# Gate and up product of a SwiGLU block moved from VectorE to ScalarE and GpSimd

## What is computed

```python
gate, up = _split(rms_norm(x, norm_ffn[i]) @ w_gate_up[i], (D_FF, D_FF))   # 2048 -> 2 * 5632
x = x + (jax.nn.silu(gate) * up) @ w_down[i]                               # 5632 -> 2048
```

## Time and profile before

| | us |
|---|---|
| median of 3 runs | 2177.11 (2175.9 to 2177.83) |
| the profiled execution | 2178.24 |
| its span, first to last instruction | 2176.4 |
| TensorE busy (share of the span) | 2158.2 (99%) |
| VectorE busy | 1555.4 (71%) |
| ScalarE busy | 1095.3 (50%) |
| GpSimd busy | 58.4 (3%) |

### The profile page before, as it was taken

The page is one execution under the profiler, slowest core; times in us unless marked ns, Lnnn a source line. Parts: engine busy times, 40 slices in busy tenths (PEclk is TensorE's granted clock), DMA queues, the critical chain, the costliest instruction groups (busy, mean ns, idle before and its releaser), DMA issues.

```text
span 2176.4 us, 29853 instructions
## 1 busy us (share of the span) xinstructions
PE 2158.2 (99%) x10052; PEld 1784.3 (82%) x10052; DVE 1555.4 (71%) x1937; ACT 1095.3 (50%) x1414; POOL 58.4 (3%) x99
## 2 busy tenths in 40 slices
PE   8999999999999999999999999999999999999999
PEld 6888888888888888888888888888878888888887
DVE  6657766888888885555566767677888888874443
ACT  7755654545555554444444444454454545544332
POOL 2101100000000000000100000000000000000000
PEclk9999999999999999999999999999999999999999
DMA  8765466667666666666555656566676666666664
GB/s 313 233 194 155 138 211 204 202 194 222 202 206 214 214 217 199 205 205 202 177 172 164 202 158 191 172 206 209 195 221 203 205 208 217 201 219 218 202 203 133
DMA packets 244569, 435.57 MB, mean 200 GB/s; under 512 B 23040, under 2 KB 43648, under 8 KB 244480
## 3 DMA queue, kind: packets, MB, share of 16 engines
q1 hardware_dynamic: 243392, 432.31, 63.7%
q10 hardware_dynamic: 1088, 2.10, 0.2%
HBM read 411.25 MB, written 2.10 MB: 190 GB/s over the span
## 4 chain that ended last, share of the span: by engine, by line
PE 70%; DVE 11%; issue 7%; SPq 6%; DMA 4%; ACT 2%; DVEq 1%; ACTq 0%
PE unit_bank L1801 52%; SPq L408 5%; PE mix_bank L1853 4%; PE mix_bank L1801 4%; DMA raw<-in_w_gate_up 4%; PE unit_bank L1853 3%; DVE w_lo L1074 3%; PE unit_bank L1813 1%; PE mix_bank L1813 1%; PE mix_bank L1871 1%; DVE sums L1096 1%; ACT w_hi L615 1%; PE mix_bank L2001 1%; DVE up_ff L1574 1%; DVE act_ff L1598 1%
## 5 line engine op out<-in xcount | busy, mean ns | idle before, releaser
L1074 DVE TENSOR_TENSOR w_lo<-raw,w_hi 128x1024 fp32r<-128x1024 f32 x687 | 828.8, 1220 | 472.8 <-ACT w_hi L615 450.7
L615 ACT ACTIVATE w_hi<-raw 128x1024 fp32r<-128x1024 f32 x687 | 719.0, 1057 | 603.4 <-PE unit_bank L1801 381.9
L1801 PE MATMUL unit_bank<-w_hi,gT_hi 128*128 128x512 f32 x704 | 217.1, 389 | 1.3 <-issue 1.3
L1801 PE MATMUL unit_bank<-w_lo,gT_hi 128*128 128x512 f32 x704 | 216.9, 389 | 0.0
L1801 PE MATMUL unit_bank<-w_hi,gT_lo 128*128 128x512 f32 x704 | 216.8, 389 | 0.0
L1801 PE MATMUL unit_bank<-w_hi,hT_hi 128*128 128x512 f32 (+1 forms) x576 | 181.2, 396 | 0.0
L1801 PE MATMUL unit_bank<-w_hi,hT_lo 128*128 128x512 f32 (+1 forms) x576 | 176.2, 387 | 0.0
L1801 PE MATMUL unit_bank<-w_lo,hT_hi 128*128 128x512 f32 (+1 forms) x576 | 175.9, 387 | 0.0
L1801 PEld LDWEIGHTS unit_bank<-w_hi,gT_hi 128*128 128x128 f32 x704 | 132.0, 188 | 29.4 <-issue 2.0
L1801 PEld LDWEIGHTS unit_bank<-w_lo,gT_hi 128*128 128x128 f32 x704 | 132.2, 188 | 27.5
L1801 PEld LDWEIGHTS unit_bank<-w_hi,gT_lo 128*128 128x128 f32 x704 | 132.2, 188 | 27.4
(11 more groups left out here) (348 smaller groups left out, 3113.9 us busy)
## 6 DMA issues: line engine op xcount, KB each, us to landing
raw<-in_w_gate_up SPq DMA_DIRECT2D x352, 512.0 KB, 4.2
raw<-in_w_down SPq DMA_DIRECT2D x176, 512.0 KB, 4.6
raw<-in_w_in_b SPq DMA_DIRECT2D x104, 512.0 KB, 4.0
raw<-in_w_o SPq DMA_DIRECT2D x64, 512.0 KB, 4.4
raw<-in_w_in_a SPq DMA_DIRECT2D x40, 512.0 KB, 3.9
moved<-turned SPq DMA_DIRECT2D x528, 32.0 KB, 2.6
raw<-in_w_mem_kv SPq DMA_DIRECT2D x31, 512.0 KB, 5.6
tanh_ff<-act_ff SPq DMA_DIRECT2D x112, 32.0 KB, 3.3
```

The source lines that it names most:

```text
L615: act.activation(w_hi[:, s, :, :], raw[:, s, :, :], ACT.Copy).then_inc(sems["hi_ready"], 1)
L1074: dve.tensor_tensor(w_lo[:, s, :, :], raw[:, s, :, :], w_hi[:, s, :, :].bitcast(F32), ALU.subtract).then_inc(sems["lo_ready"], 1)
L1801: ins = pe.matmul(all_banks[2 * pair + tile][:, 0:cols], stationary[part][:, kt + j, tile * P:(tile + 1) * P], b[:, s, j, 0:cols], start=o ...
```

## The change

ScalarE does one more operation per gate tile: after the tanh it scales `act_ff` in place by `half_rs2`. GpSimd then multiplies `up_ff` by it in place, once the up sums are complete. VectorE's `gate_silu` is gone, and `times_up` has one operation per tile, `up_ff` = (tanh + 1) * `up_ff`, with waits for the tanh and for GpSimd.

```diff
+            def up_times_gate():
+                pool.wait_ge(sems["shared_free"], t.next("shared_free"))
+                for s in range(TILES):
+                    pool.wait_ge(sems["gate_scaled"], t.next("gate_scaled"))
+                    pool.tensor_tensor(up_ff[:, s, :], up_ff[:, s, :], act_ff[:, s, :], ALU.mult).then_inc(sems["up_gated"], 1)
+
+            def gated_chunks():
+                with t.loop(0, CHUNKS_FF // 2, {"shared_free": 2, "gate_scaled": 2 * TILES}):
+                    for half in range(2):
+                        up_times_gate()
+                up_times_gate()
...
             token_rs("x_squares", sum_sq, rs, "rs_ready")
+            gated_chunks()
...
                         act.activation(tanh_ff[:, s, :], act_ff[:, s, :], ACT.Tanh,
                                        scale=half_rs[:, s:s + 1]).then_inc(sems["tanh_ff_ready"], 1)
+                        act.activation(act_ff[:, s, :], act_ff[:, s, :], ACT.Copy,
+                                       scale=half_rs2[:, s:s + 1]).then_inc(sems["gate_scaled"], 1)
...
-                def gate_silu():
-
+                def times_up():
                     for s in range(TILES):
                         dve.wait_ge(sems["tanh_ff_ready"], t.next("tanh_ff_ready"))
-                        ins = dve.scalar_tensor_tensor(out=tanh_ff[:, s, :], in0=tanh_ff[:, s, :], scalar=1.0,
-                                                       in1=act_ff[:, s, :], op0=ALU.add, op1=ALU.mult)
-                    ins.then_inc(sems["dve_chain"], 1)
-
-                def times_up():
-                    dve.wait_ge(sems["dve_chain"], t.next("dve_chain"))
-                    dve.wait_ge(sems["shared_free"], t.value("shared_free"))
-                    for s in range(TILES):
-                        ins = dve.scalar_tensor_tensor(out=up_ff[:, s, :], in0=up_ff[:, s, :],
-                                                       scalar=half_rs2[:, s:s + 1], in1=tanh_ff[:, s, :], op0=ALU.mult,
-                                                       op1=ALU.mult)
+                        dve.wait_ge(sems["up_gated"], t.next("up_gated"))
+                        ins = dve.scalar_tensor_tensor(out=up_ff[:, s, :], in0=tanh_ff[:, s, :], scalar=1.0,
+                                                       in1=up_ff[:, s, :], op0=ALU.add, op1=ALU.mult)
                     ins.then_inc(sems["dve_chain"], 1)
                     dve.wait_ge(sems["dve_chain"], t.next("dve_chain"))
                     turn_quads(up_ff)
...
                     for i in chunk_pieces():
-                        if i == 1:
-                            gate_silu()
                         if i == 5:
                             times_up()
```

More of the change, by code:

```diff
@@ L352, in trunk @@
             + ["raw_lo_ready", "sum_ready", "sum_hi_ready", "sum_lo_ready", "own_free", "shared_free",
-               "first_copied", "gate_sum", "form_ready"]
+               "first_copied", "gate_scaled", "up_gated", "gate_sum", "form_ready"]
             + ["tanh_ff_ready", "tanh_q_ready", "tanh_gate_ready", "gate_used", "rung_ready", "early_ready"]
@@ L1661, in projection_ffn @@
                     for i in pieces(len(FF_KTS), tail=layer == 1 and c == BLOCKS - 1):
-                        if c == 0 and i == 1:
-                            gate_silu()
                         if c == 0 and i == 5:
@@ L1681, in _ @@
                                                     "sum_hi_ready": 2 * 3 * len(SEVEN), "first_copied": 2, "own_free": 2,
-                                                    "shared_free": 2, "dve_chain": 2 * 4}
+                                                    "shared_free": 2, "dve_chain": 2 * 3, "up_gated": 2 * TILES}
             dve.wait_ge(sems["rs_ready"], t.next("rs_ready"))
```

## The result

| | before | changed |
|---|---|---|
| median, us | 2177.47 (2175.9 to 2178.12, 4 runs) | 2193.08 (2191.53 to 2193.61, 4 runs) |
| ratio to before | | 1.0072, 95% interval 1.0054 to 1.0089 |
| span of the profiled execution, us | 2176.4 | 2191.1 |

A forecast was written before the change was run, and what follows sets the result against it. A round through VectorE, SyncE's moves and loads was taken to set the pace, 0.60 us above TensorE's 42.16. 1.07 - 0.13 + 0.0 = +0.94 us over 18 chunks gave +16.9 us, median 2194.0; range 2172 to 2213.

The forecast's parts named there:

- What bounds the kernel: In the two chunk loops, a round through VectorE, SyncE's moves and loads takes 42.76 us, 0.60 more than TensorE needs.
- TensorE as the bound: Rival: ScalarE gets by, no conflict, and the loops run at TensorE's pace; 2163.9 us, chance 0.14.
- nearly the whole loss: Claim that 0.56 of 0.66 us lost per chunk lies at the first seven-product step, where a matmul waits for `sums_lo`.
- Part 1 and 2: Before the three-block split: removing `gate_silu` from VectorE yields only 0.02 of 1.20 us; ScalarE's two copies cost 0.0.
- Part 3: VectorE's `times_up` takes 680 instead of 744 ns, twice a chunk: -0.13 us in the loop.
- Part 4: GpSimd's two multiplications, 1.07 us each: the first fits the hole `gate_silu` left, the second costs 1.07 us a chunk.
- How near the first multiplication came: GpSimd's first multiplication was to run from 507.24 to 508.31, just ahead of L1094 at 508.34, at no cost.
- The sum: All parts together: 1.07 - 0.13 + 0.0 = +0.94 us a chunk, over 18 chunks +16.9 us.
- No conflict: Rival: GpSimd alone yields and VectorE is not held, leaving -0.15 us a chunk; 2174.4 us, chance 0.24.
- Both paid: Rival: both GpSimd multiplications cost in full, 2.01 us a chunk, +36 us; 2213.3 us, chance 0.12.
- The gap before the first `sums_hi` matmul: Sign that the forecast is right: TensorE's gap there near 1.5 us.
- The longer operation: Sign: one VectorE operation per chunk, L1112 or one behind it, longer or later by about 1 us.

The follow-up runs named there:

- experiment 1: Changed kernel with both of GpSimd's multiplications cut to 8 of 512 columns; 2174.55 us, ratio 0.9988 to the kernel before.
- Experiment 6: Kernel before with SyncE's 16 moves of a chunk spread as 4, 4, 4, 4 behind pieces 11, 12, 13, 15; 2167.29 us, ratio 0.9951.
- experiment 2: Changed kernel with each of ScalarE's two copies replaced by one of 8 columns on other data; 2192.37 us, ratio 1.0068 to the kernel before.
- experiment 5: Changed kernel with a third GpSimd multiplication per chunk, the second tile's repeated; 2212.99 us, ratio 1.0163 to the kernel before.
- experiment 3: Changed kernel with the second of GpSimd's two multiplications per chunk cut to 8 columns, the first whole; 2174.88 us, ratio 0.9987 to the kernel before.

## Why the prediction was right

Where the time of a round went, averaged over the 18 rounds inside the loops, worked out from the starts in VectorE's timelines (us):

```
from ... to                                before   changed   GpSimd short (1)
gate sum -> three-block w_lo                 4.78      4.77      4.77
three-block w_lo -> sums                     1.67      2.25      1.68
sums -> up product (times_up)                7.27      7.75      7.27
up product -> transpose                      1.44      1.32      1.32
transpose -> second three-block w_lo         5.33      5.46      5.45
second w_lo -> shared_products              15.05     14.81     14.80
shared_products -> next gate sum             7.26      7.26      7.26
round                                       42.79     43.62     42.55
```

- **What bounds the kernel.** The reading of the round was right: a chain through VectorE, SyncE and the loads, without TensorE, 0.6 us above TensorE's 42.16. Experiment 6 comes within 3.4 us of the 2163.9 that the prediction gave for TensorE as the bound, by an edit to SyncE's queue alone. The profile put 1.8 us of TensorE's own waits down to `sums_lo` where the pace of the matmuls showed 13.2 lost. But "nearly the whole loss" at the first `sums_hi` matmul was read from one chunk, whose step of 0.79 us is the longest of 18. On average the step was 0.51 us, 0.28 above the unhindered 0.23, of the 0.63 that a round loses; with the change it is 1.44, and with the spread moves 0.23. The forecast doesn't use this reading, so it cost nothing.
- **Part 1 and 2.** The gate sum to `w_lo` distance is 4.77 us after 4.78. ScalarE took VectorE's place as the one that is last, as worked out to 0.02 us; this time all 18 L1112 wait for it. That it came out so well is partly luck. The copies take 0.62 us each from start to start and not 0.57, so L650 starts 2.51 us after the first tanh on average and not 2.40, and at +3.23 us from the gate sum where L634 had +3.14. L1112 follows it after 1.55 us on average, where L1094, for which VectorE was mostly still busy, came after 1.65 and the prediction took 1.61. The two differences of 0.1 us cancel.
- **Part 3.** -0.12 us a round for `times_up`, with -0.13 forecast.
- **Part 4.** One multiplication is paid and one is free, as forecast; which operation pays varies. The price is 0.58 + 0.48 = 1.06 us a round, from the table, against 1.07. That these agree is partly luck: 1.07 was meant as the length of a multiplication, and the trace has 1.28. VectorE pays less than that, since GpSimd's row begins up to 0.1 us before L1112's and its hold is over about 0.14 us before the row ends. The doubt between the rows and the Trainium skill's page "SBUF — State Buffer", section "SBUF: two separate sides", is settled for this pair: whichever starts first keeps the other out until it is done, as that section's exclusive lock has it, by the starts at +4.69 and +4.78 us against GpSimd's +4.72. The estimate of 1.11 us by the Trainium skill, "GPSIMD Engine Reference", section "Performance versus the Vector engine", was a little nearer to 1.28.
- **How near the first multiplication came.** It was placed at 507.24 to 508.31, just ahead of L1094 at 508.34; from that chunk's gate sum this is +3.61 to +4.68 and +4.71. The trace has it end at +4.76 with L1112 at +4.69 or +4.78, and experiment 2 shows its hold end at +4.62, so it missed L1112 by some 0.07 us. The prediction let both be paid in full if the first were still running then. Experiment 2 shows that this is not so: where the two meet, `w_lo` is longer by the rest of the operation only, at most 0.17 us there.
- **The sum.** +0.94 a round was forecast, +0.83 came. The difference is a small gain of 0.12 us between the transpose and the next shared products that no step of the prediction has. It is there in experiment 1 too, so it isn't GpSimd's. It may be the shift of the transpose against SyncE's loads; that was not tried, and its cause stays open. 18 x 0.83 = 14.9 us.
- **The rivals.** "No conflict" is experiment 1's time, 2174.4 forecast for 2174.55, and it fell by experiment 1's comparison. "Both paid" was forecast at 2213.3, and experiment 5 has 2212.99, but that near agreement tests nothing: it has three multiplications, the two holds in half of its rounds, and the stretches at the lower clock. "TensorE as the bound" wasn't reached by the change, since ScalarE stands directly behind VectorE.

Three of the signs that the prediction named were half right. The gap before the first `sums_hi` matmul, forecast near 1.5 us, is 1.2 us on average (the step of 1.44 less the unhindered 0.23). The longer operation is L1112 in only 10 of 18 rounds; in the other 8 it is the one behind it. And the round is 43.6 us, not 43.7.

## What to carry to other kernels

Before work goes from VectorE to GpSimd, look at what VectorE does while GpSimd runs: an idle engine is not a free one if its operations keep VectorE's two-input operations waiting. In these runs it was free as far as VectorE was idle for about that long, and that hole is to be counted in microseconds per round. And where the profile shows TensorE at 99% busy with few waits, compare its pace with the unhindered pace of the same matmuls; here that found 13 us, of which an edit to the order of small DMAs returned 11.

## What the runs showed of the hardware

- A GpSimd multiplication of 128 x 512 f32 with two inputs takes 1.28 us alone. VectorE's two-input operation that meets it is recorded as started and takes 1.08 to 1.13 us longer where the two meet from the start: 2.84 and 2.89 against 1.76, 2.32 against 1.22. It is longer only by what is left of GpSimd's operation: in the changed kernel L1112 ends 7.62 or 7.63 us after the gate sum in all ten rounds where it is held, whether it started at +4.78 (2.84 us) or at +5.22 (2.41 us).
- Whichever starts first goes first. When L1112 started 4.69 us after the gate sum, GpSimd's operation, recorded from +4.72, waited for all of it; at +4.78 L1112 was held. The waiting GpSimd operation then got in before the next VectorE operation in all 8 rounds, though VectorE's queue had no gap.
- GpSimd's operations on 8 columns cost VectorE next to nothing. In experiment 1 they run while VectorE is idle. In experiment 3 the short one waits behind L1112 in 7 rounds of 18 and gets in before the sums, and the longest sums take 1226 ns (shortest, median and longest, by line):

```profile
L1114 DVE TENSOR_TENSOR sums<-raw x40: 1212/1220/1226, 380.5 to 1909.7; 128x1024 f32<-128x1024 f32 x40
```

- The time for which VectorE is held counts as busy. VectorE's busy time fell by 6 us where up to 30 us of work had left.
